# Channel mixer of an encoder layer: edge columns inside the first block's pass, one edge operation per step, the next block's transposes spread over a block

## What is computed

```
h2 = rmsnorm(x, norm_pre_ffn)
up = jnp.einsum('bsd,df->bsf', h2, w_up)            # 1024 -> 2 x 4096
up = centred_depthwise_conv(up, conv_w, conv_b)     # xp[:, :-2]*w[0] + xp[:, 1:-1]*w[1] + xp[:, 2:]*w[2] + bias
act = jax.nn.gelu(up[..., :D_FF]) * up[..., D_FF:]
ff = jnp.einsum('bsf,fd->bsd', act, w_down)         # 4096 -> 1024
return x + rmsnorm(ff, norm_post_ffn)
```

## Time and profile before

| | us |
|---|---|
| median of 3 runs | 6146.57 |
| lowest run | 6135.68 |
| span of the profiled execution (slowest core) | 6118.4 |
| spans of the 8 cores in it | 6082.9 to 6118.4 |
| TensorE busy | 5367.0 (88%) |
| ACT busy | 3034.0 (50%) |
| DVE busy | 2950.1 (48%) |
| POOL busy | 1752.1 (29%) |
| mean granted clock of TensorE, all cores | 0.950 to 0.953 |

### The profile page before, as it was taken

One profiled execution on the slowest core, in us unless ns is written; L12 is line 12 of the kernel. 1 busy time (PEld: TensorE's weight loads), 2 busy tenths in 40 slices (PEclk: granted clock), 3 DMA queues, 4 the chain that ended last, 5 costly groups with the idle time before them and its releaser, 6 DMA issues.

```text
span 6118.4 us, 90189 instructions; the slowest of 8 cores (6082.9 to 6118.4 us)
## 1 busy us (share of the span) xinstructions
PE 5367.0 (88%) x26761; PEld 2487.7 (41%) x26761; DVE 2950.1 (48%) x4175; ACT 3034.0 (50%) x6330; POOL 1752.1 (29%) x1846
## 2 busy tenths in 40 slices
PE   6675488888888888299999999999999999999999
PEld 2333233333333333144444444444444444444444
DVE  4565234333333333156655555665555556655554
ACT  3643223332333232166655555666555566655555
POOL 0121133233323333123323222233222222323223
PEclk8888799999999999599999999999999999999999
DMA  3698622122212211834433333343333334433333
GB/s 94 195 125 85 124 90 77 58 90 90 70 65 90 90 57 63 217 127 145 152 114 130 128 128 128 131 152 127 129 129 128 127 129 144 152 115 131 128 128 107
DMA packets 267141, 716.99 MB, mean 117 GB/s; under 512 B 86916, under 2 KB 98180, under 8 KB 265772
## 3 DMA queue, kind: packets, MB, share of 16 engines
q1 hardware_dynamic: 166556, 590.21, 29.7%
q0 software_dynamic: 100112, 121.03, 9.0%
HBM read 653.90 MB, written 111.15 MB: 125 GB/s over the span
## 4 chain that ended last, share of the span: by engine, by line
PE 73%; DVE 7%; issue 5%; DMA 5%; ACT 5%; POOL 4%; another core or an unknown queue 1%; DVEq 0%; SPq 0%; ACTq 0%; POOLq 0%
PE psum L435 53%; PE psum L913 19%; DVE arena L426 3%; ACT arena L390 2%; DMA arena<-wups 1%; DMA arena<-xf 1%; POOL arena L655 1%; DVE arena L442 1%; DMA yscr<-arena 1%; PE psum L421 1%; DMA x1s<-arena 1%; DVE arena L652 1%; ACT arena L692 1%; ACT arena L441 1%; DVE arena L671 1%
## 5 line engine op out<-in xcount | busy, mean ns | idle before, releaser
L435 PE MATMUL psum<-arena 128*128 128x512 bf16 (+3 forms) x19713 | 4085.8, 366 | 455.3 <-DVE arena L442 78.7
L435 PEld LDWEIGHTS psum<-arena 128*128 128x128 bf16 x19713 | 1854.3, 99 | 2660.6 <-issue 676.0
L888 DVE SCALAR_TENSOR_TENSOR arena<-psum,arena 128x511 f32<-128x511 f32 x2560 | 1745.4, 743 | 669.7 <-ACT arena L875 657.4
L869 ACT ACTIVATE arena<-psum,arena 128x510 f32<-128x510 f32 x1280 | 996.7, 779 | 343.9 <-PE psum L435 337.0
L894 POOL TENSOR_TENSOR arena<-arena 128x512 bf16<-128x512 bf16 x640 | 744.8, 1164 | 1459.4 <-ACT arena L892 1440.8
L913 PE MATMUL psum<-arena 128*128 128x512 bf16 x5120 | 1145.5, 387 | 0.0
L913 PEld LDWEIGHTS psum<-arena 128*128 128x128 bf16 x5120 | 509.9, 100 | 624.9 <-issue 44.5
L875 ACT ACTIVATE arena<-psum,arena 128x1 f32<-128x1 f32 x2560 | 757.3, 350 | 2.2 <-DVE arena L827 2.2
L426 DVE TENSOR_TENSOR arena<-psum,arena 128x1024 bf16<-128x1024 bf16 (+1 forms) x241 | 294.3, 1221 | 506.0 <-PE psum L421 495.2
L692 ACT ACTIVATE arena<-psum 128x512 bf16<-128x512 f32 x400 | 239.3, 598 | 526.6 <-PE psum L435 526.6
L412 ACT ACTIVATE arena<-arena 128x1024 bf16<-128x1024 f32 (+1 forms) x241 | 266.4, 1144 | 432.5 <-PE psum L421 308.5
(11 more groups left out here) (44 smaller groups left out, 1497.9 us busy)
## 6 DMA issues: line engine op xcount, KB each, us to landing
arena<-wups SPq DMA_DIRECT2D x672, 512.0 KB, 4.1
arena<-xn SPq DMA_DIRECT2D x160, 512.0 KB, 7.7
arena<-x1s SPq DMA_DIRECT2D x160, 512.0 KB, 6.4
arena<-xf SPq DMA_DIRECT2D x80, 512.0 KB, 4.5
x1s<-arena POOLq DMA_DIRECT2D x80, 512.0 KB, 6.9
y<-arena POOLq DMA_DIRECT2D x80, 512.0 KB, 4.6
wups<-w_up POOLq DMA_DIRECT2D x64, 256.0 KB, 35.9
arena<-yscr SPq DMA_DIRECT2D x20, 512.0 KB, 12.2
```

Of the source, the lines that this page charges most:

```text
L435: ins = e.matmul(out, lhsT=l, rhs=r, start=(i == 0), stop=(i == n - 1))
L869: P.op("act", lambda e, cbuf=cbuf, b=b, w1=w1, bb=bb: e.activation(out=cbuf[:, 1:511], in_=bank(b)[:, 1:511], func=AF.Identity, bias=bb, s ...
L888: P.op("dve", lambda e, o_=o_, i_=i_, wt=wt: e.scalar_tensor_tensor(out=o_, in0=i_, scalar=wt, in1=o_, op0=ALU.mult, op1=ALU.add), reads=[ ...
```

## The change

Four parts, all in phase C.

1. **Halo.** The separate stage for `haloU` is gone. In block 0, step `j` first computes the 2 x 40 halo columns of its own w_up tile into bank 7, and DVE multiplies them by the weights of the outer taps into `haloU[:, :, j, :]`. The conv bias is no longer in `haloU`.
2. **Edges.** ACT writes all 512 columns of each half in one operation. The two edge columns of both halves are then corrected by one POOL operation on 128x2x2 elements that adds `haloU`. The buffers of the two halves are one tile, `cgv`.
3. **Next block.** `pre_a` and `pre_b` are replaced by pieces: loads at step 0, squares behind steps 4, 7, 10, 13, factors behind 13, casts behind 16, 19, 22, 25, transposes and copy behind 18, 21, 24, 27 of the block ahead. `h2T` is tracked by tile.
4. **Start.** Block 0's x loads come before those of the neighbour tokens, which have a buffer of their own (`xr[0]`). w_down is loaded in eight parts, at steps 0, 4, ..., 28 of block 0, and tracked by part.

```diff
+        def wdload(q):
+            P.op("pool", dma1(wd[:, q * 4:(q + 1) * 4, :],
+                              w_down[q * 512:(q + 1) * 512, :].rearrange("(j p) d -> p j d", p=128)),
+                 writes=[("wd", q)], ndma=1)
...
-        for side in range(2):
-            hv = haloU[:, :, side * NBLK:(side + 1) * NBLK]
...
-            P.op("dve", lambda e, hv=hv, wsd=wsd: e.tensor_tensor(out=hv, in0=hv, in1=wsd, op=ALU.mult),
-                 reads=["haloU", "cst"], writes=["haloU"])
-            P.op("dve", lambda e, hv=hv, cbb=cbb: e.tensor_tensor(out=hv, in0=hv, in1=cbb, op=ALU.add),
-                 reads=["haloU", "cst"], writes=["haloU"])
...
+        def pre_load(i):
+            for t in range(4):
+                P.op("sp", dma1(xt[t], src[i * BLK + t * 128:i * BLK + (t + 1) * 128, :]), writes=[("cxt", t)],
+                     ndma=1)
...
+        pre_load(0)
+        for t in range(4):
+            pre_square(0, t)
+        pre_scale(0)
+        halo_pre()
+        for t in range(4):
+            pre_cast(0, t)
+            pre_turn(0, t)
+
+        def halo(j, sl):
+            w = wup[sl]
+            hp = bank(7)[:, 0:2 * NH]
+            for half in range(2):
+                mm_group(hp[:, half * NH:(half + 1) * NH],
+                         [(w[:, kc, half, :], hhT[:, kc, :]) for kc in range(8)],
+                         reads=[("wup", sl), "hhT"], writes=[("ps", 7)])
+            P.op("dve", lambda e: e.tensor_tensor(
+                out=haloU[:, :, j, :].rearrange("p h (s i) -> p h s i", s=2),
+                in0=hp.rearrange("p (h s i) -> p h s i", h=2, s=2),
+                in1=cw4[:, :, j, 0:3:2].unsqueeze(3).broadcast_to([128, 2, 2, NBLK]), op=ALU.mult),
+                reads=[("ps", 7), "cst"], writes=[("hu", j)])
...
                 ensure_loaded(n + NW - 1)
-                sl = wslot[n]
+                if i == 0 and j % 4 == 0:
+                    wdload(j // 4)
+                if j == 0 and more:
+                    pre_load(i + 1)
+                sl = n % NW
                 w = wup[sl]
+                if i == 0:
+                    halo(j, sl)
...
-                    P.op("act", lambda e, cbuf=cbuf, b=b, w1=w1, bb=bb: e.activation(
-                        out=cbuf[:, 1:511], in_=bank(b)[:, 1:511], func=AF.Identity, bias=bb, scale=w1),
-                        reads=[("ps", b), "cst"], writes=[(cn, k, "m")])
-                    for side in range(2):
-                        col = 511 * side
...
+                    P.op("act", lambda e, half=half, b=b, c=c, cv2=cv2: e.activation(
+                        out=cv2[:, half, :], in_=bank(b), func=AF.Identity, bias=cst[:, C_CB + c:C_CB + c + 1],
+                        scale=cst[:, C_CW + 3 * c + 1:C_CW + 3 * c + 2]),
+                        reads=[("ps", b), "cst"], writes=[("cgv", k, half)])
+                P.op("pool", lambda e, cv2=cv2, i=i, j=j: e.tensor_tensor(
+                    out=cv2[:, :, 0:512:511], in0=cv2[:, :, 0:512:511], in1=haloU[:, :, j, i:NH:NBLK], op=ALU.add),
+                    reads=[("hu", j), ("cgv", k, 0), ("cgv", k, 1)], writes=[("cgv", k, 0), ("cgv", k, 1)])
...
+                if more:
+                    if j in (4, 7, 10, 13):
+                        pre_square(i + 1, (j - 4) // 3)
+                    if j == 13:
+                        pre_scale(i + 1)
+                    if j in (16, 19, 22, 25):
+                        pre_cast(i + 1, (j - 16) // 3)
+                    if j in (18, 21, 24, 27):
+                        pre_turn(i + 1, (j - 18) // 3)
...
-            if i + 1 < nblk:
-                nxt = pre_a("c", tiles_for(i + 1), xt, EPS)
...
-                if t == 1 and nxt is not None:
-                    pre_b(nxt, xs, 0, gpf)
```

154 lines of the change are left out of this document (79 added, 75 removed).

## The result

The changed kernel took 5953.98 us in the median of 4 runs (lowest 5945.85). Its ratio to the kernel before, measured beside it, is 0.9691, 95% interval [0.966, 0.9722]: faster by 3%. (In some executions of every kernel, here two of the kernel before near 7000 us, a die has a lower granted clock throughout; the ratios leave these out, and the experiments are read on cores that it did not touch.) The forecast was 5962 us, 0.970 of the median before.

The account below looks back on a forecast made before the run. TensorE, busy 88% of the span, was taken as the bound. First block -63.5, common blocks -122 and last block +0.6 gave -185: span 5933, with 28 us around it 5962 us; range 5935 to 6015.

Parts of the forecast that it names:

- the 28 us around the span: Outside the profiled span: 28 us between span 6118.4 and median 6146.6, carried over unchanged into the forecast time.
- the price of nothing for the half clock behind the grown wait: Block start, step 2: wait grows from 1.58 to 2.2 us, 0.6 a block, with no clock loss added.
- the 122 forecast: Blocks 1 to 18: moving the next block's turns out of the down pass gains 122 us in all.
- The sum of 169.7 us: Common block: 165.7 of matmuls, 1.8 for turns, 2.2 of waiting make 169.7 us, against 176.5 before.
- rival 3: Block start: the longer wait at step 2, or the next, brings half clock, 2.1 us on 19 blocks; 6002; chance 0.08.
- the 63.5 forecast: First block: start 27, up pass 148, down pass 55 make 230 us, 63.5 less than before.
- its chain: First block's up pass: halo matmuls wait for DVE's multiply until +8.1 us, so two steps take 8.8 us.
- the piece of 16 short matmuls: First block's up pass: each step's halo matmuls add 0.69 us, making 4.14 us where TensorE is alone.
- The turns in front of the multiply: First block's up pass: four turns stand ahead of DVE's halo multiply, 1.2 us each, 5 in all.
- rival 4: First block: halo waits keep the clock at half, or w_up tiles come late; +125 us, 6087; chance 0.13.
- The edge: Each up-pass step: POOL's add on four elements takes 0.2 us, with no loss in a common step.
- ACT as the bound: Up pass: function changes between Gelu and Square might hold ACT; 2.5 us each gives 6319; summed as zero; chance 0.05.

Follow-up runs that it names:

- the last experiment: The changed kernel with DVE's scaling of the last down tile ahead of step 0's four DVE operations, rerun on another chip: ratio 0.9621 to the kernel before.

## Where the prediction was right, and which steps of it failed

The total held, and it held by luck: two steps failed with opposite sign, the 28 us around the span (26 too many) and the price of nothing for the half clock behind the grown wait (18.5 too few). With the 5 us of the first block these terms put the forecast 13 us too high; the profiled execution took 5945.85 us, 16 less than forecast.

**What lies around the span: wrong, 26 us.** "28 us lie around the span and I carry them over unchanged". In the profiled execution of the changed kernel 1.6 us do (5945.85 against a span of 5944.3). The 28 us were no part of the program: they were the difference between the profiled execution of the kernel before and the median of others. Beside the last experiment that kernel took 6124 to 6148, each time 1.5 to 3.2 us over the span of its slowest core. By spans alone the forecast was 5933, and 5944.3 came.

**Common blocks: 19 us less than the 122 forecast.** The sum of 169.7 us was exact for the blocks in which the clock stays up: 169.70. The waits are as summed: 2.15 at step 2 (9.06 for 6.91 of work; forecast 2.2), none at step 4, 0.45 for a turn, 55.25 for the down pass. The step that failed is that the sum left the clock at 1.00 behind the longer wait, and the weight of rival 3. I gave 0.08 to the half clock behind the longer wait, with the reason that "1.4 us there left the clock at 1.00". That is a statement on 1.4, and the sum itself had 2.2. It came in 11 of 18 blocks, with 1.68 us instead of the 2.1 put down: 18.5 us. The kernels with the scale moved forward show that the half clock needs this wait, since 28 and 60 us came back where the wait alone accounts for 13 and 41 (19 x 0.66 and 19 x 2.15). They do not show that a wait of this length is enough: 2.15 us with the turns in the down pass brought none.

**First block: 5 us more than the 63.5 forecast.** It took 225.2 us (forecast 230). The start was 29.4 instead of 27, since the square of the neighbour tokens started 15.3 us behind the first issue and not 11. ACT on the slowest core, first stretch of phase C (the SP rows are the loads of block 0's x and of the neighbour tokens):

```profile
2465.55 1.75 SPq L345 DMA_DIRECT2D arena<-x1s  x4
2467.34 1.49 SPq L835 DMA_DIRECT2D arena<-x1s  x4
2468.77 1.06 ACT L792 ACTIVATE arena<-arena 128x1024 bf16<-128x1024 f32 x1 [18.05 <-DMA arena<-x1s]
...
2480.89 1.06 ACT L838 ACTIVATE arena<-arena 40x1024 bf16<-40x1024 f32 x1 [5.65 <-DMA arena<-x1s]
```

Block 0's own rows are squared 3.2 us behind their issue; the 40 neighbour rows come 12 us behind the end of theirs, without w_down beside them, and ACT waits 5.65 us for them. I had taken the 15.2 us of before for the work of full DMA engines, and part of it is this load's own. The pass was 140.5 instead of 148: 4.21 us a step instead of 4.4. The mechanism (bank 7 every second step) was right, and its chain was right in size: from a step's first up matmul to the halo matmuls that wait for the next multiply it is 8.01 us (2536.20 to 2544.21), against +8.1. The term that was mis-sized is the piece of 16 short matmuls. The 0.69 us were read where the clock was at half; in the pass it was at 1.00. Windows of TensorE, the kernel before in the stage for the halo columns (ten pieces in 6.92 us), then the two steps from 2535.79 in the changed kernel:

```profile
2560.00:2580.00 20.00, 6.92 (x160) 0.50 1.02 369
2535.70:2544.20 8.50, 7.97 (x64) 1.00 1.01 225
```

Behind the wait the up matmuls now start 0.41 us behind the start of the piece (2535.79 to 2536.20), not 0.69: two steps take 8.01 + 0.41 = 8.42 us and not 8.8, 6 us over the pass. The turns in front of the multiply cost 0.5 beyond the common wait and not 1.2. w_down's parts land after 10.6 us, and the w_up tiles cost TensorE 0.8 us in two waits: rival 4 did not come. The experiment with odd steps in bank 0 shows how near it was: with the pace only a little higher, the same tiles are late by 0.9 to 3.2 us.

**The edge: right.** 208 ns in the mean over 640, against 0.2 taken and 1.04 as the upper bound. The kernel with the edge 1.16 us later shows what hung on this choice: 50 us.

**ACT as the bound: right.** A Square (L792, 2519.86) stands 0.52 us behind the start of a Gelu (L933, 2519.34) in the up pass, so the change of function costs nothing. The Trainium skill, "ScalarE: Activation LUTs", section "What ACT_TABLE_LOAD costs", gives about 2.66 us for every switch to a different table set; the 0.52 us here leave no room for one, as the sum had it.

**What the parts are worth.** The forecast booked 122 us to "the turns leave the down pass" and no gain to the edge operation, only a cost. The kernels bear out both as far as they go: with the turns put back 128 to 133 us are lost, and with the edge operation alone a block is 1.0 us longer. Whether the moved turns also need the room that the edge operation made on ACT is not shown. The text says that ACT "loses four edge activations" and then has 2.2 us of work a step, but it does not work out the step with them: 2.99 us of 3.45, which the earlier trace rows give, and 1.4 us of room in three steps for a piece of 1.04 to 1.15. By these numbers the pieces would have fitted, narrowly. The run that put four activations back took 163 us more because ACT's step was 3.63 us in it, which is dearer than in the kernel before.

## What to carry to other kernels

Before work is moved under the cover of the critical engine, work out the time per step of the engine that does it, from start to start: here 2.99 us of 3.45 left room for a piece every third step, and 3.63 left none. When a part of a change is taken back for a test, check in the trace that it costs what it cost before: here two small activations went from 0.59 to 0.80 us by names that made them wait for each other, and the test could not say what it was meant to say. Read the granted clock beside every duration that a sum uses. A wait that grows on TensorE should be priced with the clock behind it, and it can often be taken out for nothing by letting the operation that frees a PSUM bank go ahead of work that nobody waits for yet: here that gave another 0.7%. And compare spans with spans: here a profiled execution and the median of other runs lay 28 us apart, of which under 2 us were time around the span.

## What the runs showed of the hardware that was not expected

- The half clock behind a wait of the same length comes and goes. With 1.99 us ahead of step 2 it comes in 9 to 11 of 18 blocks, nearly in every second one. In the kernel with the turns in the down pass waits of 1.94 (core 7) and 2.15 us (core 2) at the same place were followed by full speed in every block, while the clock fell at the turns; in the kernel with four edge activations a wait of 1.87 us was too. What else decides it was not settled.
- Many short waits do not bring it: in the first block TensorE has 14 waits for the multiply of the halo columns, 8.8 us in all and mostly 0.45 us every 8.42, and the granted clock is 1.00 from 2506 to 2635.
- 16 short matmuls of 40 columns take 0.69 us in single groups at a granted clock of 0.50, and 128 in a row 4.47 us at the same clock, 0.56 per 16: part of the 0.69 is the end of the last one. At 1.00 the next matmul starts 0.41 us behind the first of the 16.
- Semaphore waits of ACT on itself have a price: activations of one column start 0.24 us apart where none waits for the other, and 0.45 us apart where each does (2908.63 and 2909.08 in the kernel with four edge activations).
